# PEER's gates spread by float32r products in two parts, and the routing's comparisons and key products in PSUM

## The reference, cut to what matters

```python
def peer_ffn(hn, wq, subkeys, down, up):
    q = (xt @ wq).reshape(N, H, 2, PEER_DKEY // 2)              # N = 256 tokens, H = 8 heads
    s = jnp.einsum('nhpd,hpkd->nhpk', q, subkeys)               # scores of 2 x 128 keys
    s_half, i_half = lax.top_k(s, K)                            # K = 16
    cand_s = s_half[:, :, 0, :, None] + s_half[:, :, 1, None, :]
    cand_i = i_half[:, :, 0, :, None] * PEER_NKEYS + i_half[:, :, 1, None, :]
    top_s, pos = lax.top_k(cand_s, K)
    eidx, gate = take_along_axis(cand_i, pos), softmax(top_s)
    ...
    act = gelu(einsum('cd,chkd->chk', xc, down[ec])) * gc
    return einsum('chk,chkd->cd', act, up[ec])
```

## Time and the profile before

| | |
|---|---|
| three runs | 2661.12, 2662.39, 2662.99 us, median 2662.39 |
| the profiled execution's own time | 2663.43 us |
| its span, first to last instruction | 2661.6 us |
| PE busy | 2453.2 us (92%) |
| DVE busy | 1789.8 us (67%) |
| ACT busy | 1172.1 us (44%) |
| POOL busy | 759.3 us (29%) |
| chain that ended last | PE 79%, DVE 9%, ACT 4%, POOL 4%, DMA 2% |
| of that chain, the products that spread gates (line 1998) | 4% |
| one-hots: lines 1979 and 1982 | 128 each, 155.1 and 248.0 us of DVE |

### The profile page before, as it was taken

One profiled execution on the slowest core, in us unless ns is written; L12 is line 12 of the kernel. 1 busy time (PEld: TensorE's weight loads), 2 busy tenths in 40 slices (PEclk: granted clock), 3 DMA queues, 4 the chain that ended last, 5 costly groups with the idle time before them and its releaser, 6 DMA issues.

```text
span 2661.6 us, 38829 instructions
## 1 busy us (share of the span) xinstructions
PE 2453.2 (92%) x15906; PEld 2213.1 (83%) x15906; DVE 1789.8 (67%) x2832; ACT 1172.1 (44%) x1950; POOL 759.3 (29%) x358
## 2 busy tenths in 40 slices
PE   6978988999999999998878888799999999999998
PEld 5876988999999888886757777589999999888886
DVE  4564558978887555555777275467987888555555
ACT  3354344444444444444443444244444444444443
POOL 3000004986665000000000053202896666100000
PEclk8888999999999999998888989899999999999999
DMA  5422434554545666663322343145554444566664
GB/s 168 122 84 64 126 105 143 172 162 147 147 144 150 184 189 189 189 187 107 121 86 88 119 130 116 49 148 161 164 170 150 145 150 143 169 188 189 188 186 124
DMA packets 108279, 383.33 MB, mean 144 GB/s; under 512 B 12975, under 2 KB 15840, under 8 KB 107528
## 3 DMA queue, kind: packets, MB, share of 16 engines
q1 hardware_dynamic: 108104, 380.86, 46.8%
HBM read 379.74 MB, written 1.06 MB: 143 GB/s over the span
## 4 chain that ended last, share of the span: by engine, by line
PE 79%; DVE 9%; ACT 4%; POOL 4%; DMA 2%; issue 1%; SPq 0%; DVEq 0%; ACTq 0%; POOLq 0%
PE psum L370 22%; PE psum L371 21%; PE psum L372 21%; PE psum L1998 4%; POOL weight_parts L349 3%; PE psum L402 2%; ACT weight_parts L338 1%; DVE weight_parts L343 1%; PE psum L2644 1%; PE psum L2414 1%; PE psum L607 1%; PE psum L1457 1%; PE psum L1018 1%; PE psum L501 0%; PE psum L1357 0%
## 5 line engine op out<-in xcount | busy, mean ns | idle before, releaser
L349 POOL TENSOR_TENSOR weight_parts<-weight_ring,weight_parts 128x1024 fp32r<-128x1024 f32 x276 | 697.1, 2533 | 591.5 <-ACT weight_parts L338 591.0
L370 PE MATMUL psum<-acts_high,weight_parts 128*128 128x256 f32 x2768 | 819.6, 296 | 46.2 <-DVE weight_parts L343 19.5
L371 PE MATMUL psum<-acts_low,weight_parts 128*128 128x256 f32 x2768 | 793.4, 287 | 0.0
L372 PE MATMUL psum<-acts_high,weight_parts 128*128 128x256 f32 x2768 | 793.0, 286 | 0.0
L338 ACT ACTIVATE weight_parts<-weight_ring 128x1024 fp32r<-128x1024 f32 x681 | 713.8, 1049 | 162.8 <-PE psum L372 65.6
L343 DVE TENSOR_TENSOR weight_parts<-weight_ring,weight_parts 128x1024 fp32r<-128x1024 f32 x405 | 496.7, 1228 | 312.8 <-ACT weight_parts L338 312.2
L370 PEld LDWEIGHTS psum<-acts_high,weight_parts 128*128 128x128 f32 x2768 | 541.4, 196 | 61.9 <-DVE weight_parts L343 21.2
L371 PEld LDWEIGHTS psum<-acts_low,weight_parts 128*128 128x128 f32 x2768 | 542.0, 196 | 2.7 <-issue 1.7
L372 PEld LDWEIGHTS psum<-acts_high,weight_parts 128*128 128x128 f32 x2768 | 541.0, 195 | 0.0
L370 PE MATMUL psum<-weight_parts,peer_coef 128*128 128x512 f32 x1024 | 405.8, 396 | 4.0 <-issue 3.9
L372 PE MATMUL psum<-weight_parts,peer_coef 128*128 128x512 f32 x1024 | 405.7, 396 | 0.0
(11 more groups left out here) (422 smaller groups left out, 2883.5 us busy)
## 6 DMA issues: line engine op xcount, KB each, us to landing
weight_ring<-in_peer_down SPq DMA_DIRECT2D x128, 512.0 KB, 3.6
weight_ring<-in_peer_up SPq DMA_DIRECT2D x128, 512.0 KB, 3.6
weight_ring<-in_peer_u SPq DMA_DIRECT2D x128, 512.0 KB, 3.6
weight_ring<-in_peer_v SPq DMA_DIRECT2D x128, 512.0 KB, 4.1
weight_ring<-in_w_in SPq DMA_DIRECT2D x88, 512.0 KB, 3.7
weight_ring<-in_w_out SPq DMA_DIRECT2D x16, 512.0 KB, 3.6
weight_ring<-in_peer_w_q SPq DMA_DIRECT2D x16, 512.0 KB, 3.6
weight_ring<-in_w_in_v SPq DMA_DIRECT2D x10, 512.0 KB, 4.0
```

What stands on the lines that cost most here:

```text
L349: q.e.tensor_tensor(self.low, self.ring, self.high.bitcast(F32), ALU.subtract).then_inc(*self.unit.ready.once())
L370: q.e.matmul(out, sh, mh, start=first, stop=False)
L371: q.e.matmul(out, sh, ml, start=False, stop=False)
L372: return q.e.matmul(out, sl, mh, start=False, stop=last)
```

## The change

Four edits go together, in both PEER layers.

1. **The gates' products.** The gates are split in a float32r part and a rest (`gates_high`, `gates_low`). `Onehots` marks the first key in a float32r tile, the second key in PSUM bank 6, and writes two products of that mark: times `gates_high` (DVE) and times `gates_low` (ACT, four instructions, in a second phase of the step). `Spread` is then one float32r product of 128x256 for each token instead of one float32 product of 128x128, and fills two banks. `ApplyGates` has to add the halves: ACT copies the high half to SBUF, DVE adds the low one in two instructions and multiplies.
2. **The routing's `eq` and `part`** and the gates lie in PSUM instead of SBUF, and the row 0 to 15 is read from PSUM.
3. **Both tiles' scores** have their own area, and the second tile's score product comes before unit 2 instead of unit 12. DVE begins only when both tiles' scores are copied.
4. **The places**: the second phase of both tiles stands before unit 36 instead of 42, the third before unit 38 instead of 45, and the first one-hots before unit 41 instead of 48. GELU has banks 4 and 5 only.

```diff
@@ Route.vector
-        q.wait_ge(self.scores_kept)
+        q.wait_ge(r.scores_kept, r.iota_copied)
...
-            settle(c, q, "vector", q.e.tensor_tensor(r.eq, over(r.partf, TOPK, 3), r.iota16, ALU.is_equal))
-            settle(c, q, "vector", q.e.tensor_tensor(r.eq, r.eq, over(r.idxf[:, :, a, :], TOPK, 2), ALU.mult))
-            q.e.tensor_reduce(self.res[:, a, :, :], r.eq, AX, ALU.add)
+            settle(c, q, "vector", q.e.tensor_tensor(self.eq, over(r.partf, TOPK, 3), self.iota16, ALU.is_equal))
+            settle(c, q, "vector", q.e.tensor_tensor(self.eq, self.eq, over(r.idxf[:, :, a, :], TOPK, 2), ALU.mult))
+            settle(c, q, "vector", q.e.tensor_reduce(self.res[:, a, :, :], self.eq, AX, ALU.add))
@@ Route.__init__
+        self.eq = c.bank(0, 4).rearrange("p (h a b) -> p h a b", h=PEER_H, a=TOPK)
+        self.gates = c.bank((6, 3)[i])[:, 0:P].rearrange("p (h k) -> p h k", h=PEER_H)
+        small = c.bank(7).rearrange("p (x h k) -> p x h k", x=4, h=PEER_H)
+        self.part = small[:, 1, :, :].bitcast(U32)
+        self.iota16 = over(over(c.bank(7)[:, 0:TOPK], TOPK, 1), PEER_H, 1)
@@ Onehots
-        q.e.tensor_tensor(self.hot, over(over(self.c.bank(7)[:, 0:P], GROUP, 1), 2, 1),
-                          over(x.pairs[:, :, tokens], P, 3), ALU.is_equal).then_inc(*self.marked.once())
+        q.wait_ge(*self.hot_free, x.routed, x.iota_copied, self.low_before)
+        q.e.tensor_tensor(ones, iota, over(x.pairs[:, 1, tokens], P, 2), ALU.is_equal).then_inc(*self.marked.once())
+        q.e.tensor_tensor(self.first, iota, over(x.pairs[:, 0, tokens], P, 2), ALU.is_equal)
         q.wait_ge(self.marked)
-        q.e.tensor_tensor(self.hot[:, 0, :, :], self.hot[:, 0, :, :], over(x.gates[:, tokens], P, 2), ALU.mult).then_inc(*self.ready.once())
+        q.e.tensor_tensor(self.second[:, :, 0, :], ones, over(x.gates_high[:, tokens].bitcast(F32), P, 2),
+                          ALU.mult).then_inc(*self.high.once())
+
+    def scalar(self, q):
+        x = self.x
+        yield
+        q.wait_ge(self.high, *self.hot_free)
+        for t in range(GROUP):
+            token = GROUP * self.g + t
+            last = q.e.activation(self.second[:, t, 1, :], self.c.bank(6)[:, P * t:P * t + P], ACT.Copy, bias=0.0,
+                                  scale=x.gates_low[:, token:token + 1])
+        last.then_inc(*self.low.once())
@@ Spread
-            out = self.c.bank(self.b)[:, P * t:P * t + P]
-            last = q.e.matmul(out, self.hot[:, 0, t, :], self.hot[:, 1, t, :], start=True, stop=True)
+            out = self.c.bank(self.b, 2)[:, 2 * P * t:2 * P * t + 2 * P]
+            last = q.e.matmul(out, self.onehots.first[:, t, :], self.onehots.second[:, t, :, :].rearrange("p a n -> p (a n)"),
+                              start=True, stop=True)
@@ ApplyGates
     def scalar(self, q):
+        q.wait_ge(self.spread, self.copy_free)
+        q.e.activation(self.copy, self.high, ACT.Copy).then_inc(*self.copied.once())
+
+    def vector(self, q):
...
+        q.e.tensor_tensor(self.high[:, 0:there, :], copy[:, 0:there, :], self.low[:, 0:there, :],
+                          ALU.add).then_inc(*self.added.once())
+        q.e.tensor_tensor(kept, copy[:, there:NKEYS, :], self.low[:, there:NKEYS, :],
+                          ALU.add).then_inc(*self.stored.once())
+        q.wait_ge(self.added)
+        q.e.tensor_tensor(dst, dst, self.high[:, 0:there, :], ALU.mult).then_inc(*self.applied.once())
@@ peer
-        places = {2: routes[0:1], 14: routes[1:2], 44: routes, 47: routes}
+        places = {2: routes[0:1], 4: routes[1:2], 38: routes, 40: routes}
-        c.rotation = [4, 5, 6]
+        c.rotation = [4, 5]
-            n_groups, made, used, first = T // GROUP, 0, 0, 49
+            n_groups, used, finished, first = T // GROUP, 0, 0, 42
```

More of the change, by code:

```diff
@@ L1854, in scalar @@
         c, r = self.c, self.r
-        q.wait_ge(self.scored, *self.scores_free)
+        q.wait_ge(self.scored)
         if r.half_dim == 64:
             for a in range(2):
-                last = q.e.activation(r.scores[:, :, a, :], c.bank(2 * a, 2).rearrange("p (h n) -> p h n", h=PEER_H),
+                last = q.e.activation(self.scores[:, :, a, :], c.bank(2 * a, 2).rearrange("p (h n) -> p h n", h=PEER_H),
                                       ACT.Copy)
         else:
-            last = q.e.activation(r.scores, c.bank(0, 4).rearrange("p (h a n) -> p h a n", h=PEER_H, a=2), ACT.Copy)
+            last = q.e.activation(self.scores, c.bank(0, 4).rearrange("p (h a n) -> p h a n", h=PEER_H, a=2), ACT.Copy)
         last.then_inc(*self.scores_kept.once())
@@ L1864, in scalar @@
         q.wait_ge(self.shifted)
-        q.e.activation(self.res[:, 2, :, :], self.res[:, 2, :, :], ACT.Exp).then_inc(*self.powers.once())
+        q.e.activation(self.gates, self.gates, ACT.Exp).then_inc(*self.powers.once())
     def top16(self, q, vals, idx, src):
@@ L1937, in cut @@
             return view.rearrange(f"p ({' '.join(names)}) -> p {' '.join(names)}", **dict(zip(names, shape)))
-        self.scores = cut(PEER_H, 2, NKEYS)
+        self.scores = [cut(PEER_H, 2, NKEYS) for _ in range(NT)]
         self.cand = cut(PEER_H, TOPK, TOPK)
-        self.eq = cut(PEER_H, TOPK, TOPK)
         self.vals = cut(PEER_H, 2, TOPK)
@@ L1968 @@
 class Onehots(Step):
+    phases = 2
     def __init__(self, c, x, g):
-        self.c, self.x, self.g, self.hot = c, x, g, x.hot[:, g % 2, :, :, :]
-        self.hot_free = x.hot_free[g % 2]
-        self.marked, self.ready = c.mark("keys_marked"), c.mark("gate_onehots")
+        self.c, self.x, self.g = c, x, g
+        self.first, self.second = x.first[:, g % 2, :, :], x.second[:, g % 2, :, :, :]
+        self.hot_free, self.low_before = x.hot_free[g % 2], x.low_made
+        self.marked, self.high, self.low = c.mark("keys_marked"), c.mark("gate_high"), c.mark("gate_low")
+        self.ready = [self.high, self.low]
+        x.low_made = self.low
@@ L1976, in vector @@
     def vector(self, q):
         x, tokens = self.x, slice(GROUP * self.g, GROUP * self.g + GROUP)
[L1978 to L1980 removed]
+        iota, ones = over(self.c.bank(7)[:, 0:P], GROUP, 1), self.c.bank(6).rearrange("p (t n) -> p t n", t=GROUP)
+        q.wait_ge(*self.hot_free, x.routed, x.iota_copied, self.low_before)
@@ L2006, in __init__ @@
     def __init__(self, c, x, g, spread):
-        self.x, self.g, self.spread, self.there = x, g, spread.spread, x.there
-        self.gates = c.bank(spread.b).rearrange("p (t n) -> p n t", t=GROUP)
-        self.stored = x.stored = c.mark("gates_stored")
+        self.c, self.x, self.g, self.spread, self.there = c, x, g, spread.spread, x.there
+        gates = c.bank(spread.b, 2).rearrange("p (t a n) -> p a n t", t=GROUP, a=2)
+        self.high, self.low = gates[:, 0, :, :], gates[:, 1, :, :]
+        self.copy, self.copy_free = x.copy, x.copy_free
+        self.copied = c.mark("gates_copied")
+        self.added, self.stored = c.mark("gates_added"), c.mark("gates_stored")
+        x.copy_free = self.stored
         self.applied = x.applied = c.mark("gates_applied")
+        x.stored = self.stored
         x.gated = GROUP * (g + 1)
@@ L2150, in peer @@
         x.experts = c.sb(name + "_experts", [P, NKEYS, T], ctx)
-        x.pairs = c.sb(name + "_pairs", [P, 2, T], ctx)
-        x.gates = c.sb(name + "_gates", [P, T], ctx)
+        x.gates_high = c.sb(name + "_gates_high", [P, T], ctx, F32R)
+        free = work[:, :, :].rearrange("p k t -> p (k t)")
+        x.pairs, x.gates_low = free[:, 0:2 * T].rearrange("p (a t) -> p a t", a=2), free[:, 2 * T:3 * T]
+        x.copy = free[:, 3 * T:3 * T + GROUP * NKEYS].rearrange("p (n t) -> p n t", t=GROUP)
         first_kept = 70
@@ L2191, in peer @@
                     used += 1
+                while finished < len(onehots):
+                    c.plan(onehots[finished])
+                    finished += 1
             c.low_by = "vector"
```

58 lines of the change are left out of this document (27 added, 31 removed).

## The result

| | before | after |
|---|---|---|
| median | 2661.84 us (2661.12 to 2662.99, 4 runs) | 2615.59 us (2613.73 to 2620.72, 4 runs) |
| ratio after to before | | 0.9829, 95% interval 0.9812 to 0.9846 |
| span of the profiled execution | 2661.6 us | 2613.7 us |
| last GELU of the down stage, layer 1 and 2 | 860.56, 2281.53 us | 836.75, 2233.55 us |

The account below looks back on a forecast made before the run. PE was taken to bound the gates, with DVE and PE nearly tied in the routing. Layer 1 gains 22.5 us and layer 2 21.7, together 44.2: 2662.4 - 44.2 = 2618.2, say 2618 us, range 2604 to 2642.

Parts of the forecast that it names:

- Rival 5: Spread on PE: float32r products of one-hots cost what float32 ones did, 0.88 us a group; 2669 us, chance 0.03.
- 3: Rounds among the gates lose to the loop PE, ACT, DVE, 0.15 us in each of 128 groups; 2637 us, chance 0.10.
- rival 4: Among the gates DVE becomes the bound; gain gone at a 4.5 us round, 2725 us at 5.0; chance 0.05.
- DVE's routing: Routing: moving operands to PSUM avoids waits for POOL's instructions, taking 21.1 us a layer off DVE's 130.1 and 129.6.
- Rival 2: Routing: comparisons in PSUM save DVE less; 2660 us if nothing, 2639 if half; chance 0.14, most near 2639.
- The rest: After unit 37, ACT waits for DVE at the powers and PE rests 11 us, layer 1 from 534.9 to 546.25.
- rival 6: No rest of PE between units 37 and 38; 69.7 us off, 2593 us; needs DVE 11 us earlier; chance 0.06.
- The clock: After PE's rest the clock runs at half for 3.3 us, adding 1.65 us of work in each layer.
- The sum: Unit 127 ends at 837.8 in layer 1, 22.5 us off, and 2259.55 in layer 2, 21.7 off; together 44.2.
- Cover among the gates: Among the gates DVE's mean round of 3.15 us stays hidden under PE's 3.36, helped by units without a group.
- the rule on PSUM's fixed cost: Skill's errata: a PSUM source costs DVE 0.065 us more per instruction; a round of seven 0.45 us longer, forecast still standing.
- ACT among the gates: Among the gates ACT's rounding, GELU, copy and four instructions take 3.24 us a round at most, under PE's 3.36.

Follow-up runs that it names:

- d: The changed kernel with the routing's second and third phase before units 40 and 42 and the first one-hots before unit 45; 2591.11 us.
- e: The changed kernel, but DVE starts each tile on that tile's own scores and waits for both only ahead of `eq`; 2596.06 us.
- f: The changed kernel plus one unused 512-column DVE instruction per round, between the first key's mark and the product with the high gates; 2666.59 us.
- g: The changed kernel plus an unused 512-column DVE instruction per round, placed behind the product with the high gates; 2619.12 us.
- j: The changed kernel plus an unused 512-column DVE instruction before the high product, with the first key's mark moved behind that product; 2618.68 us.

## Why the prediction was right, and where it was not

**The spread: right.** "0.40 x 64 = 25.6 us in each layer": 0.48 against 0.89 us a group in the trace, and 50.5 and 50.6 us in the two kernels that isolate it. Rival 5 is out, and so are 3 and 4, since PE is full among the gates.

**DVE's routing: right.** "21.1 us a layer" came out as 22.7 and 22.1, since line 1913 too fell, to 1.95 and 0.30 us for the two tiles, where 2.50 us stood for each: 2.8 us that the prediction had left to chance. The small lines took 0.29 us where "0.23" was forecast. Rival 2 is out (1910 and 1911 at 2.3 us).

**The rest: right in mechanism, 2 us too long.** ACT waits 9.0 us at the powers instead of "some 11", because DVE ended at 541.69, not 542.35, and ACT came to the wait later than forecast: unit 35's GELU was at 530.74, not 529.1. DVE itself started 0.9 late, at 434.25, and its shorter routing made up for it; 0.7 of the 0.9 lay ahead of the change, as the first score product came at 420.55 instead of 419.88. The stop of PE, "534.9", was counted from a GELU and not from the product's end 0.30 earlier, and was at 536.3 in the trace. PE's restart, forecast for 546.25, was at 545.42. Only the restart enters the sum. Kernels d and e have no rest and measure 2591 and 2596, around the 2593 of rival 6.

**The clock: right in the sum, by luck in its length.** "1.65 us of work" was 2.2 in layer 1: from the restart at 545.42 to the end of unit 38 (0.30 before its GELU, 550.49) are 5.07 us, 2.19 over a unit's 2.88. In layer 2 it was 1.6 (4.48 us for the unit). I took the length of the low stretch from 3.3 us after a short pause. Here it was some 10 us in both layers, but it began in the middle of the rest. Only what was left of it at the restart cost work, 5.0 us in layer 1 and 3.6 in layer 2.

**The sum.** Layer 1 ended 860.56 - 836.75 = 23.8 us earlier (forecast 22.5), layer 2 another 24.2 (forecast 21.7), 48.0 in all against 44.2. The rows divide the difference. In layer 1 the restart was 0.8 us earlier than forecast, the clock cost 0.5 more, and from there to the end of unit 127 PE took 836.45 - 545.42 - 2.19 = 288.8 us instead of 259.2 + 30.7 = 289.9: 1.1 less, as rounds of 3.34 instead of 3.36 give for 64 groups. In layer 2, with everything shifted by the 24.0 us by which its first score product came earlier (1816.45 instead of 1840.47), the restart was 1.2 earlier, the clock as forecast and the pace again 1.1 less. That is 1.4 and 2.3 us; 0.2 more came between the layers. The earlier restarts are DVE's shorter routing.

**Cover among the gates: the outcome right, the reason wrong.** The step "Every fourth unit or so has no group ..., so DVE needs 64 x 3.15 = 202 us in PE's ... 273. It stays hidden", and with it rival 4's "4.5 us" as the point from which DVE decides, failed: by it the 3.75 us of f would have stayed hidden, and they cost 51 us. DVE's mark for a group may not be written before ACT has read the last one from bank 6, and ACT's four in turn wait for DVE's high product. The bound is this ring, and it leaves 0.2 us, not 1.1. Free units cover only what stands outside it, as in g and j. The forecast held because 3.16 is under 3.36, which I had not worked out; on this point it was luck. I did see the two halves of it (the four "to be done 2.88 us after the spread before", and "the four on ACT wait" if DVE is late), but not that DVE waits for them too. The same step puts a false sum behind the rule on PSUM's fixed cost. By it a round of seven was to be 0.45 us longer and the forecast to "stand under either". Three of the seven lie in the ring, and 3 x 0.065 = 0.2 us, an estimate from the figures of the Trainium skill, VectorE: DVE Perf Modes, section The TRN2 errata, would have used up all of its slack. The trace shows no such cost on these instructions: 0.68 to 0.70 us for 512 columns with an input in PSUM, and 0.68 to 0.69 with both in SBUF (lines 978 and 1736 of the kernel before).

**ACT among the gates: right within 0.1 us.** The four take 1.14 us together against 1.08, and ACT's gap in a round is 0.16 to 0.28 us where 3.36 - 3.24 = 0.12 was the least that I allowed. The copy of 512 columns stood in that sum with 0.62; by the prediction's own two points it is 0.57, and it took 0.60.

## What to carry to other kernels

An engine's busy share, and even its mean round against the bound's round, does not say that it is hidden. Follow each buffer that has only one copy from writer to reader and back to the writer: that ring must be shorter than the round, on its own, and work can be taken out of it by order alone. Pauses in the plan, such as the units without a group, cover late work outside the ring but not inside it. A stretch of work that was made shorter pays only if what waits for it isn't moved forward by more; look for the places once more after the parts are in. Before a small loss in a window is explained, see whether the stage ends inside the window. And a price of contention read from a full pipeline is an upper bound where its own delay stops the other engine.
